# TensorE's order of work in the expert loop of a mixture-of-experts kernel: the scatter product split around the down product

## The reference, cut to what matters

```python
hid = jax.nn.silu(jnp.einsum('td,edf->tef', t, we_g)) * jnp.einsum('td,edf->tef', t, we_u)
routed = jnp.einsum('tef,efd->td', hid * combine[..., None], we_d)
```

## Time and profile before

| | |
|---|---|
| median of 3 runs | 1085.79 us |
| lowest and highest | 1085.4 and 1090.15 us |
| the profiled execution, its own time | 1084.99 us |
| its span in the profile | 1083.2 us |
| mean granted clock of TensorE | 0.98 |
| TensorE busy (matmul) | 1010.3 us, 93% |
| VectorE busy | 444.9 us, 41% |
| ScalarE busy | 210.0 us, 19% |
| the expert loop | from 500.23 us to 1065.9 us of the span |

### The profile page before, as it was taken

The page is one execution under the profiler, slowest core; times in us unless marked ns, Lnnn a source line. Parts: engine busy times, 40 slices in busy tenths (PEclk is TensorE's granted clock), DMA queues, the critical chain, the costliest instruction groups (busy, mean ns, idle before and its releaser), DMA issues. The chain is left out here.

```text
span 1083.2 us, 11628 instructions
## 1 busy us (share of the span) xinstructions
PE 1010.3 (93%) x4426; PEld 481.6 (44%) x4461; DVE 444.9 (41%) x915; ACT 210.0 (19%) x396; POOL 49.8 (5%) x63
## 2 busy tenths in 40 slices
PE   3999999999999998699999999999999999999982
PEld 1757644665555443344433333333333333333440
DVE  0102420460011124644455455455455455455566
ACT  2111201200000101312222222222222222222322
POOL 0100000000000000010000000000000000000000
PEclk9799999999999999799999999999999999999997
DMA  9972023204042566615999999999999999999941
GB/s 340 380 284 78 1 98 135 97 1 155 1 155 78 181 237 212 241 61 234 421 418 421 420 419 420 420 420 419 417 418 419 417 418 413 413 419 402 380 168 60
DMA packets 67865, 300.27 MB, mean 277 GB/s; under 512 B 6800, under 2 KB 8976, under 8 KB 41056
## 3 DMA queue, kind: packets, MB, share of 16 engines
q1 hardware_dynamic: 61024, 281.51, 65.2%
q0 software_dynamic: 6784, 17.99, 4.5%
HBM read 302.29 MB, written 3.77 MB: 283 GB/s over the span
## 5 line engine op out<-in xcount | busy, mean ns | idle before, releaser
L895 PE MATMUL bank<-ring,QK 128*64 128x512 f32 x1024 | 225.3, 592 | 2.0 <-DMA ring<-in_w_exp_up 1.0
L895 PEld LDWEIGHTS bank<-ring,QK 128*64 128x64 f32 x1024 | 74.3, 137 | 147.8 <-issue 147.8
L924 PE MATMUL bank<-Fm,VG 128*128 128x512 bf16 x544 | 123.1, 379 | 11.7 <-issue 8.0
L633 PE MATMUL bank<-hT,ring 128*128 128x384 f32 x384 | 126.8, 486 | 2.2 <-DVE QK L1428 1.2
L1620 DVE TENSOR_TENSOR hT<-bank,hT 128x512 f32<-128x512 f32 x204 | 126.4, 685 | 3.4 <-PE bank L968 2.3
L917 PE MATMUL bank<-ring,VG 128*64 128x512 f32 x512 | 116.9, 598 | 0.5 <-ACT VG L1181 0.5
L633 PEld LDWEIGHTS bank<-hT,ring 128*128 128x128 f32 x384 | 72.7, 190 | 52.7 <-DVE QK L1428 1.4
L924 PEld LDWEIGHTS bank<-Fm,VG 128*128 128x128 bf16 x576 | 53.9, 97 | 71.3 <-issue 6.4
L673 PE MATMUL bank<-ring,hT 128*128 128x512 f32 x192 | 82.6, 592 | 0.0
L1629 DVE TENSOR_TENSOR Fm<-bank,Fm 128x512 f32<-128x512 f32 x64 | 44.3, 692 | 90.0 <-ACT Fm L1188 90.0
L1188 ACT CAST Fm<-bank 128x512 bf16<-128x512 f32 x64 | 37.4, 585 | 214.7 <-PE bank L917 214.7
(11 more groups left out here) (316 smaller groups left out, 815.8 us busy)
## 6 DMA issues: line engine op xcount, KB each, us to landing
ring<-in_w_exp_gate SPq DMA_DIRECT2D x69, 1024.0 KB
ring<-in_w_exp_up SPq DMA_DIRECT2D x69, 1024.0 KB
ring<-in_w_exp_down SPq DMA_DIRECT2D x69, 1024.0 KB
ring<-in_w_ada SPq DMA_DIRECT2D x12, 2048.0 KB, 12.7
ring<-in_w_in SPq DMA_DIRECT2D x10, 2048.0 KB, 20.4
ring<-in_w_four_out SPq DMA_DIRECT2D x2, 2048.0 KB, 7.7
ring<-in_w_out SPq DMA_DIRECT2D x2, 2048.0 KB, 9.0
ring<-in_w_ret_out SPq DMA_DIRECT2D x1, 2048.0 KB, 7.8
```

The lines of the kernel that those rows point to most:

```text
L633: ins = mm(o[:, 0:T], w[:, k, m * P:(m + 1) * P], rhs[:, k, :], start=(k == 0), stop=(k == kc - 1))
L895: ins = mm(ps[0][n * SLOTS:(n + 1) * SLOTS, :], xT[:, k, n * SLOTS:(n + 1) * SLOTS], expert(2 * s + n)[0][:, k, :, :], start=(k == 0), sto ...
L924: ins = mm(ps[4 + g % 4][:, :], slotT[:, k, t * P:(t + 1) * P], y[:, h * 512:(h + 1) * 512], start=(n == 0), stop=(n == 2))
```

## The change

scatter takes the list of tiles that it issues. Its waits ahead of tile 0 are made only where tile 0 is among them; the waits ahead of tiles 2, 4 and 5 stay with their tiles. In each pass p of the loop TensorE now issues tiles 0 and 1 of scatter(p - 1), then the down product of p, then tiles 2 to 5 of scatter(p - 1). The last scatter, after the loop, runs whole. Other engines' programs are as before.

```diff
-            def scatter(p):
-                pe.wait_ge(sem("lo_ready"), 2 * (p + 1))
-                if p + 2 <= LAST:
-                    pe.wait_ge(sem("xT_ready"), 2 * (p + 2))
-                if p:
-                    pe.wait_ge(sem("summed"), 6 * p)
-                for g in range(6):
+            def scatter(p, some):
+                if 0 in some:
+                    pe.wait_ge(sem("lo_ready"), 2 * (p + 1))
+                    if p + 2 <= LAST:
+                        pe.wait_ge(sem("xT_ready"), 2 * (p + 2))
+                    if p:
+                        pe.wait_ge(sem("summed"), 6 * p)
+                for g in some:
                     if g == 2 and p + 3 < PAIRS:
                         pe.wait_ge(sem("slot_found"), p + 4)
                     if g == 2 and PAIRS <= p + 3 <= LAST:
...
                 hidden_T(p)
                 if p:
-                    scatter(p - 1)
+                    scatter(p - 1, (0, 1))
                 if p < PAIRS:
                     down(p)
                 else:
...
                     pe.wait_ge(sem("rest_ready"), 2 * p)
                     down_duo(p % 2)
-            scatter(LAST - 1)
+                if p:
+                    scatter(p - 1, (2, 3, 4, 5))
+            scatter(LAST - 1, range(6))
```

## The result

The changed kernel takes 1088.7 us (median of 20 runs, 1086.4 to 1093.49) against 1085.07 us before (20 runs, 1082.87 to 1090.15): a ratio of 1.0032, 95% interval 1.0022 to 1.0043. That is 3.6 us slower: a small loss, and the whole interval lies on its side. The forecast was 1089.1 us in a range of 1086.3 to 1092.3.

The account below looks back on a forecast made before the run. TensorE was taken to set the pace, with DMA just beside it. Switches + 8.3, stalls filled - 5.1 and loop end + 0.1 gave + 3.3 on 1084.99; with 0.8 for the median, 1089.1 us, range 1086.3 to 1092.3.

Parts of the forecast that it names:

- Two switches a pass, 0.25 us: Around the later scatter tiles: full to narrow 0.14 us in 33 passes, narrow to full 0.11 in 34; 8.3 us added.
- The first matmul's missing record: Ahead of scatter in a pair: 0.216 us of the listed 0.27 us gap is an unrecorded matmul, leaving 0.05.
- The stalls filled, 5.1 us: Passes 30 to 33: down fills scatter's waits for VectorE's copy of expert_of between tiles 1 and 2, saving 5.1 us.
- the modelled tail: At the four stalls: listed idle time starts 0.163 us after the next matmul could have started; 0.65 us more saved.
- Moved work at nothing: VectorE's later sums and the y_hi group move behind gate_up's 7 us (duos: 3.64 us and tokens); cost nothing.
- Nothing gained at the end of the loop: Ahead of the last scatter: the 3.02 us of idle time stay; VectorE's last sum may add 0.1.
- The estimate of 0.166 us: Skill page's constant that back-to-back matmuls hide, taken per switch: 11 us for two switches, net + 6.
- the open weights: At gate_up behind full tiles: the first narrow weights lie open, 0.05 us within the 0.14 of full to narrow.
- The median: Median of the runs, 1085.79 us, taken as 0.8 above the profiled execution's 1084.99 and added to the sum.
- The full tail of the pipe: Rival at both new switches in 33 passes: each waits out 0.163 us, 0.38 a pass, 1093.3 us; chance 0.12.
- the hidden switch: Rival at the switch into scatter: full-tile weights load beside the last narrow matmuls, some - 0.4 us, 1085.4; chance 0.10.
- the duos give their saving back: Rival in the duos: gathered tokens, expert weights or VectorE's chain eat half the saving, net + 5.8, 1091.6 us; chance 0.08.

Follow-up runs that it names:

- the narrow scatter: The changed kernel with each bf16 scatter matmul of a pair issued as two of 128x64 side by side: 1086.09 us, ratio 1.0005 to the kernel before.

## Why the prediction was right

*Two switches a pass, 0.25 us* (0.11 and 0.14): right to the hundredth, 16.55 against 16.29 us. It could be priced blind since both switches were already in the kernel before, at other borders: gate_up to tokens, and scatter to down. The first matmul's missing record, found from 18 weight loads against 17 matmuls, was what showed that the pairs had no stall to fill: read literally, 0.27 us a pass would have looked like 8 us of stalls. Over the loop: pass 1 is 0.21 longer, passes 2 to 29 by 28 x 0.256 = 7.17, the four passes bring - 4.24, the end + 0.13; together + 3.3, the predicted sum.

*The stalls filled, 5.1 us*: 5.1 to 5.2. Adding 0.163 a stall for the modelled tail was right; the listed idle time alone says 4.4. Pass 30 shows it by itself: 17.67 us before against an ordinary 16.29, 1.38 for a listed wait of 1.20.

*Moved work at nothing*: right in the parts that the rows show. *Nothing gained at the end of the loop*: right, the same 3.02 us.

*The Trainium skill, TensorEngine Tiling (Array Packing), section Key Properties* says that changing the tiling mode drains TensorE. The trace agrees that a change of mode costs, 0.09 to 0.11 us each, and the narrow scatter ties the cost to the mode and not to the type; that it is a drain is not shown. The estimate of 0.166 us by *the Trainium skill, TensorE: Matmul & The Clock Gate, section Single matmul latency*, would have been too dear: two of them are 0.33 a pass where 0.25 was measured with the open weights.

*The median.* The 0.8 us added for it came from three runs; by the 20 runs the kernel before is at 1085.07, and the sum gives 1088.4 for the measured 1088.7. That the loop's + 3.3 came out to the tenth is partly luck, since the terms were only known to some 0.01 us a pass.

*The rivals.* The full tail of the pipe (0.38 a pass) and the hidden switch (0.14) are refuted by 16.55. That the duos give their saving back did not come true in the changed kernel, but it was closer than I had it, and elsewhere: I looked at the gather, while the expert weights were next. The slower pairs made the room; with the saving alone, DMA took 1.9 of 4.2 us back in the profile. Had the change been made in the four passes only, I would have forecast 4 us and measured 2.4.

The one thing not weighed was that the clock may fall in the last scatter, worth 1.4 to 1.7 us in the six profiles that have it, up to half of the effect that was to be predicted.

## What to carry to other kernels

Count the borders between tile shapes of TensorE when its order is changed: one more round from full to narrow tiles and back costs 0.25 us here, the profile shows it as busy time, and a switch was free only at the place where the engine waits for other work. Cut an order where a stall is, not in every pass: the same edit is a loss of 7 us in thirty passes and a gain in four. Where one engine is 98% busy and DMA is full beside it, what makes the first faster can be paid back by the second, as it was here; a run with loads left out shows it.

## What the runs showed of the hardware that I had not expected

- bf16 matmuls in two 128x64 tiles side by side do the work of full 128x128 ones in the same time (six full: 6 x 0.216 = 1.30 us; twelve narrow: 1.29 us), and border on fp32 matmuls of the same shape with no gap.
- After an idle time of 3.02 us ahead of the last scatter the granted clock fell to its lower level in six of eleven profiles and stayed in five; the fall cost 1.4 to 1.7 us.
- Across a border of tile shapes the first weights were loaded together with the first matmul (608.96 and 608.97), within one shape 0.2 to 0.4 us ahead of it (605.66 for 605.88, 611.59 for 612.02).
